# A mixture-of-experts stage with its gate steps ahead of its up steps, and constant multiplications where TensorE stands idle

## The chip, the cores and the metric

One core of one Trainium2 chip. The metric is the device time of one execution in microseconds (us), as the median of several. The engines are named as in the profile: PE is TensorE, PEld its weight loads, DVE is VectorE, ACT is ScalarE, POOL is GpSimd, SP is SyncE, which issues most of the DMAs.

## What is computed

Two layers of a hybrid decoder for 512 new prompt positions and 8 decode tokens (520 rows of width 1024), all in float32. Each layer adds attention and convolution, and then a mixture of experts:

```python
x += W_out [ DiffAttn(h) || ConformerConv(h) ],   h = RMSNorm(x)
x += HierMoE(RMSNorm(x))

# HierMoE: each row takes the best of 4 groups, and in it the best 2 of 4 experts
hg = x @ w_gate[e]            # 1024 -> 512
hu = x @ w_up[e]              # 1024 -> 512
y  = (silu(hg) * hu * gate_weight) @ w_down[e]   # 512 -> 1024
```

There are 16 experts. Each has three matrices of 2,048 KB, which are read from HBM once in each layer.

## The kernel before, in words

The kernel is written engine by engine: each engine has its own instruction stream, in which the order is written out by hand, and the streams meet at semaphores only. Both layers run through one loop (`l`).

**Tiles.** Rows are held in 5 tiles of up to 128 (the last has the 8 decode rows). Outputs of PE go to 8 banks of 128x512 float32 numbers. The expert stage works on 13 **units**. A unit is one expert with up to 128 rows, or, for units 2, 6 and 11, a pair of experts with up to 64 rows each, whose multiplications write the upper and the lower half of the same bank.

**Routing.** PE turns the last tile and multiplies it with the router's weights (L957). DVE picks groups and experts and signals `m_ok`. PE then makes cumulative counts (L976, L978), DVE makes one-hot rows from them, PE makes row lists from these (`early_list` L987 for the first two units, `unit_list` L996 for all of them), DVE turns the lists into row numbers (L1918), and POOL gathers the rows of units 0 and 1 (L1406). `gathered(u)` on PE waits for a gather and turns the rows (transposes, all recorded at L645, the helper `turn`); DVE multiplies them with the norm's weights into `probs` (L1456, the helper `tt`).

**A unit on PE.** `gate_up(u, ks)` (L1016) runs the steps `ks` out of 8: in each step one 128x512 multiplication for gate and one for up (twice as many, half as high, for a pair), all at L1027. At its first step it waits for `xt_ok` and for all gate and up loads of the unit. After its last step a 1x1 multiplication (L1032, the **fence**) signals `gu_ps`. ACT then computes Silu of the gate bank (L1335), DVE multiplies it by the up bank (`hidden`), PE turns the product (`turn_hidden`, four transposes), ACT copies it (L1339), and `down(u)` runs 4 steps of two multiplications (L1054) and a fence (L1060). ACT and DVE scale its two banks by the gate weight (L1347, L2012), and POOL adds the rows into `x_rows` in HBM (L1417), one addition after the other; a pair needs two.

The order on PE, after unit 0, is for each u: steps 0 to 3 of unit u+1, `turn_hidden(u)`, steps 4 to 7 of unit u+1, `gathered(u+2)`, `down(u)`. Unit 0's steps are interleaved with the row lists, and `gathered(1)` stands in their middle. DVE reaches `hidden(0)` only after it has made the row numbers of all units and the lists of rows that did not fit (`spill`, L2041).

**Weights.** SP issues the 48 loads of a layer in a fixed order (L520): gate and up of each expert of a unit, then its down matrices. There are 9 slots (`ring` 0 to 5, `w_last`, `x`, `feat`), and load n goes into slot n mod 9. A load is issued when `slot_used` tells that PE has done its last multiplication from the slot; SP waits for this in order, so a load whose slot isn't free holds back all behind it. Then come the next layer's projection weights.

**Layer's end.** PE reads the number of spilled rows (none here), and waits for `layer_go`, which POOL signals after the last row addition. SP then reloads `x`, and PE's next work is to turn small parameter rows and the normed tiles.

**Bank 5**, into which the change writes, is the up bank of units 1, 3, 5, 7, 9 and 11 and an output of earlier stages.

Of the kernel before, what the change touches and what calls it, by code (L numbers as in the profile page):

```python
# [31 lines left out]
KC = D // P  # L32
# [16 lines left out]
F = 512  # L49
# [9 lines left out]
UNITS = SINGLES + (EXPERTS - SINGLES) // 2  # L59
# [14 lines left out]
def places_of(u):  # L74

    q = u + sum(1 for pair in PAIRED if pair < u)
    return [q, q + 1] if u in PAIRED else [q]
# [20 lines left out]
def slot_of(q, j):  # L98

    return loads_in_order().index((q, j)) % SLOTS_MOE  # L100
# [96 lines left out]
def hybrid_step(nc, a, o, x_rows, xn_rows):  # L197
# [17 lines left out]
    with ExitStack() as ctx:  # L215
# [3 lines left out]
        def sem(name):  # L219
            return ctx.enter_context(nc.semaphore(name))  # L220
# [11 lines left out]
        const = sb("const", [P, const_width])  # L232
# [6 lines left out]
        ones = cs("ones")  # L239
# [24 lines left out]
        xe_t = probs_flat.rearrange("p (s c n) -> p s c n", s=2, n=P)  # L264
# [64 lines left out]
        bank = [pair_bank[i // 2][:, i % 2, :] for i in range(4)]  # L329
# [101 lines left out]
        xe_in = [sem("xe_in0"), sem("xe_in1")]  # L431
        xt_ps = sem("xt_ps")
        xt_ok = sem("xt_ok")
        gu_ps = sem("gu_ps")
        silu_ok = sem("silu_ok")
        hid_ok = sem("hid_ok")
# [34 lines left out]
        def halves_of(u):  # L471

            return [slice(0, HALF), slice(HALF, P)] if u in PAIRED else [slice(0, P)]
# [168 lines left out]
        def _(pe):  # L642
# [10 lines left out]
            with pe.Fori(0, DEPTH) as l:  # L653
# [8 lines left out]
                for t in range(TILES):  # L662
                    pe.wait_ge(xn_ok, l * TILES + (1, 2, 3, 5, 4)[t])
                    for g in range(2):
                        b = 4 + 2 * (t % 2) + g
# [250 lines left out]
                def project(t, ks):  # L916
                    if t == 0 and ks[0] == 0:
                        pe.wait_ge(slot_in[5], l * 16 * loads_of(5) + 16)
                        pe.wait_ge(ot_ok, l * SAMPLE + SAMPLE - 1)
                    if t == SAMPLE - 1 and ks[0] == 0:  # L920
                        pe.wait_ge(ot_ok, l * SAMPLE + SAMPLE)
                    if t == SAMPLE and ks[0] == 0:
                        pe.wait_ge(dec_f, l + 1)
                    if t >= 2 and ks[0] == 0:
                        pe.wait_ge(x2_ok, l * TILES + t - 1)
                    for k in ks:
                        w = ring[:, 5, :] if k < 4 else w_last
                        if t == 0 and k == 4:
                            pe.wait_ge(last_in, l * 16 + 16)
                            pe.wait_ge(cat_ok, l + 1)  # L930
                        for j in range(2):
                            mm = pe.matmul(bank[2 * (t % 2) + j][rows_at(t, j), :], feat[:, k, cols(t)],  # L932
                                           w[:, (k % 4) * D + j * AW:(k % 4) * D + (j + 1) * AW],
                                           start=(k == 0), stop=(k == KC - 1))
                            if t == TILES - 1 and k == 3 and j == 1:
                                mm.then_inc(slot_used[5], 1)
                    if ks[-1] == KC - 1:
                        mm.then_inc(wo_ps, 1)
# [15 lines left out]
                def route(t):  # L954
# [3 lines left out]
                                       w_route[:, k, :], start=(k == 0), stop=(k == KC - 1))  # L958
                    mm.then_inc(log_ps, 1)

                project(0, range(KC))
                sampled_turn()
                turn_o(SAMPLE - 1)
# [7 lines left out]
                route(TILES - 1)  # L971


                pe.wait_ge(m_ok, l + 1)
                width = TILES * EXPERTS
                pe.matmul(bank[7][:, 0:width + EXPERTS], cs("before"), chosen, start=True, stop=True)  # L976
# [6 lines left out]
                def early_list(u):  # L983

                    pe.wait_ge(hot_ok, l * LISTS + u + 1)
                    for t in range(TILES):
                        mm = pe.matmul(bank[1][:, u * PAY:(u + 1) * PAY], hot[:, u % 2, t, :], pay[:, t, :],  # L987
                                       start=(t == 0), stop=(t == TILES - 1))
                    mm.then_inc(idx_ps, 1)
# [21 lines left out]
                def landed(q, j):  # L1011

                    s = slot_of(q, j)
                    pe.wait_ge(slot_in[s], l * 16 * loads_of(s) + 16 * (load_of(q, j) + 1))

                def gate_up(u, ks):  # L1016
                    b = u % 2
                    if ks[0] == 0:
                        pe.wait_ge(xt_ok, l * 2 * UNITS + u * 2 + 2)
                        for q in places_of(u):  # L1020
                            for j in range(2):
                                landed(q, j)
                    for k in ks:
                        for j in range(2):
                            for q, rows in zip(places_of(u), halves_of(u)):
                                s = slot_of(q, j)
                                mm = pe.matmul(bank[2 + 2 * b + j][rows, :], xe_t[:, b, k, rows],  # L1027
                                               slots[s][:, k * F:(k + 1) * F], start=(k == 0), stop=(k == KC - 1))
                                if k == KC - 1:
                                    mm.then_inc(slot_used[s], 1)  # L1030
                    if ks[-1] == KC - 1:
                        pe.matmul(bank[7][0:1, 0:1], ones[:, 0:1], ones[:, 0:1], start=True, stop=True)\  # L1032
                            .then_inc(gu_ps, 1)

                def turn_hidden(u):
                    pe.wait_ge(hid_ok, l * UNITS + u + 1)
# [4 lines left out]
                def down(u, ks=range(FC)):  # L1041
# [17 lines left out]
                    if ks[-1] == FC - 1:  # L1059
                        pe.matmul(bank[2 + 2 * b][0:1, 0:1], ones[:, 0:1], ones[:, 0:1], start=True, stop=True)\  # L1060
                            .then_inc(dn_ps, 1)

                for u in range(FIXED):
                    early_list(u)
                gathered(0)
                for u in range(FIXED):
                    unit_list(u)
                for k in range(KC):
                    gate_up(0, range(k, k + 1))
                    unit_list(FIXED + k)  # L1070
                    if k == KC // 2 - 1:
                        gathered(1)
                for u in range(FIXED + KC, UNITS):
                    unit_list(u)
                for u in range(UNITS):
                    if u + 1 < UNITS:
                        gate_up(u + 1, range(4))
                    if u + 1 < UNITS:
                        turn_hidden(u)
                        gate_up(u + 1, range(4, KC))  # L1080
                    if u + 2 < UNITS:
                        gathered(u + 2)
                    if u == UNITS - 2:
                        down(u, range(FC - 1))
                        turn_hidden(u + 1)
                        down(u, range(FC - 1, FC))
                    else:
                        down(u)


                pe.wait_ge(spill_ok, l + 1)
                pe.sem_inc(pe_tick, 1)
                n_spill = pe.value_load(sp_i[0:1, 0:1], min_val=0, max_val=MAX_SPILL)
# [38 lines left out]
        def _(act):  # L1132
# [10 lines left out]
            with act.Fori(0, DEPTH) as l:  # L1143
# [187 lines left out]


                def silu(u):
                    act.wait_ge(gu_ps, l * UNITS + u + 1)
                    act.activation(hid[:, u % 2, :], bank[2 + 2 * (u % 2)][:, :], ACT.Silu).then_inc(silu_ok, 1)  # L1335

                def hidden_out(u):
# [116 lines left out]
        def _(v):  # L1454
            def tt(out, in0, in1, op):
                return v.tensor_tensor(out, in0, in1, op)  # L1456
# [24 lines left out]
            with v.Fori(0, DEPTH) as l:  # L1481
# [522 lines left out]
                def hidden(u):  # L2004
                    b = u % 2
                    v.wait_ge(silu_ok, l * UNITS + u + 1)
                    tt(hid[:, b, :], hid[:, b, :], bank[3 + 2 * b][:, :], ALU.mult).then_inc(hid_ok, 1)

                def y_half(u):
# [107 lines left out]
```

## Time and profile before

| | |
|---|---|
| median of 3 runs | 1511.77 us (1511.41 to 1515.68) |
| profiled execution | 1512.05 us, of which the trace spans 1510.0 |
| PE busy | 1304.7 us (86%), 4730 instructions |
| DVE busy | 631.5 us (42%) |
| ACT, POOL busy | 230.9 us, 152.3 us |
| mean granted clock of PE | 0.92 |
| mean DMA rate | 210 GB/s |

All sums of terms are made against the profiled execution, 1512.05 us. Layer 0 is 0 to 757 us, layer 1 the rest; the expert stage of layer 0 runs from 424 to 740 us, that of layer 1 from 1172 to 1480. The granted clock is 1.00 at 2.4 GHz and 0.50 at 1.2 GHz. PE's multiplications overlap, so the length of one record is longer than the time from one to the next; times of a stage are read from the chain or from the start of the first to the start of what follows. One float32 multiplication is shown as two MATMUL records.

### The profile page before, as it was taken

Reading aid. Unit: us, or ns where it says so; the run is one execution under the profiler, and the core shown is the slowest. Engines: PE = TensorE matmul, PEld = TensorE weight load, DVE = VectorE, ACT = ScalarE, POOL = GpSimd, SP = SyncE. Lnnn points to the kernel's source line nnn. Section 1 sums busy time; section 2 is a strip of 40 time slices with the busy share of each in tenths; the row PEclk is TensorE's granted clock in tenths of the full one; section 3 lists DMA queues with packets and bytes.
Section 4 is the critical chain, followed back from the end, with each engine's and each line's share of the span. In section 5 each row is a group of like instructions: output and inputs, shape, how many; then the busy total and the mean of one; then the engine's idle time right before and its main releaser. Section 6 shows DMA issues by size and latency. Waiting matters only on the chain.

```text
span 1510.0 us, 15202 instructions
## 1 busy us (share of the span) xinstructions
PE 1304.7 (86%) x4730; PEld 632.1 (42%) x4730; DVE 631.5 (42%) x1272; ACT 230.9 (15%) x740; POOL 152.3 (10%) x79
## 2 busy tenths in 40 slices
PE   5999975889679999999569999657994899999993
PEld 3544433445333443444245444344453444444441
DVE  4579986532461110111046799866325511111100
ACT  2011323321100000000110123232301000000000
POOL 0002240000010111110100022400000001101001
PEclk9999996799889999999869999868997899999997
DMA  9501333375274998998870022324833759999973
GB/s 303 201 1 55 94 91 111 92 263 217 100 276 175 342 387 325 386 386 327 278 248 0 1 77 86 101 88 126 303 145 122 291 190 366 385 324 384 391 263 92
DMA packets 102125, 316.81 MB, mean 210 GB/s; under 512 B 10552, under 2 KB 11122, under 8 KB 101980
## 3 DMA queue, kind: packets, MB, share of 16 engines
q1 hardware_dynamic: 88576, 276.91, 49.4%
q0 software_dynamic: 8000, 24.26, 6.9%
q10 hardware_dynamic: 5468, 14.64, 2.6%
q8 instruction: 42, 0.69, 0.2%
q14 instruction: 39, 0.32, 0.1%
HBM read 292.75 MB, written 31.74 MB: 215 GB/s over the span
## 4 chain that ended last, share of the span: by engine, by line
PE 55%; DVE 18%; DMA 12%; DVEq 7%; issue 4%; SPq 1%; ACT 0%; POOLq 0%; POOL 0%; ACTq 0%
PE pair L1027 11%; PE pair L1054 9%; PE bank L1027 9%; PE pair L686 8%; PE pair L932 8%; DMA w_last<-in_w_up 6%; DVE conv L1568 4%; PE bank L645 3%; DVEq L1570 3%; DVE probs L1456 2%; DMA x_rows<-qk_t,rows_g 2%; DVE sc_dec L1629 2%; DVE conv L1552 1%; DMA ring<-in_w_up 1%; PE pair L805 1%
## 5 line engine op out<-in xcount | busy, mean ns | idle before, releaser
L1027 PE MATMUL pair<-ring,probs 128*128 128x512 f32 (+1 forms) x384 | 169.3, 629 | 9.5 <-DMA w_last<-in_w_up 7.3
L1456 DVE TENSOR_TENSOR probs<-bank,vec_g 128x512 f32<-128x512 f32 x52 | 33.5, 685 | 314.2 <-PE bank L645 314.2
L1027 PE MATMUL bank<-ring,probs 128*128 128x512 f32 (+1 forms) x352 | 147.2, 613 | 1.7 <-DMA w_last<-in_w_up 1.2
L686 PE MATMUL pair<-feat,ring 128*128 128x512 f32 x256 | 141.9, 648 | 0.9 <-DVE feat L1456 0.9
L717 PE MATMUL pair<-ring,feat 128*128 128x512 f32 (+1 forms) x320 | 135.2, 595 | 1.6 <-ACT v_rows L1194 1.6
L1054 PE MATMUL pair<-ring,v_rows 128*128 128x512 f32 (+1 forms) x320 | 126.9, 594 | 1.9 <-DVE qk_t L2012 1.9
L1390 POOL TENSOR_TENSOR w_last<-x 128x2048 f32<-128x2048 f32 x16 | 73.7, 4624 | 381.9 <-ACT x L1229 275.4
L1568 DVE SCALAR_TENSOR_TENSOR conv<-u_t,conv_w,conv 128x512 f32<-128x512 f32 x120 | 105.4, 919 | 5.2 <-issue 0.9
L1417 POOL DMA_INDIRECT x_rows<-qk_t,rows_g x32 | 49.6, 1550 | 520.6 <-DVE qk_t L2012 470.0
L1552 DVE SCALAR_TENSOR_TENSOR conv<-u_t,conv_w,conv 128x512 f32<-128x512 f32 x120 | 90.2, 751 | 17.2 <-issue 13.2
L1027 PEld LDWEIGHTS pair<-ring,probs 128*128 128x128 f32 (+1 forms) x384 | 61.7, 180 | 79.1 <-issue 71.3
L1027 PEld LDWEIGHTS bank<-ring,probs 128*128 128x128 f32 (+1 forms) x352 | 58.2, 182 | 75.8 <-issue 74.1
L2012 DVE TENSOR_SCALAR qk_t<-pair,gate 128x512 f32<-128x512 f32 x26 | 19.5, 751 | 166.8 <-PE pair L1060 90.9
L717 PEld LDWEIGHTS pair<-ring,feat 128*128 128x128 f32 (+1 forms) x320 | 50.4, 170 | 71.7 <-issue 71.6
L717 PE MATMUL bank<-ring,feat 128*128 128x512 f32 (+1 forms) x160 | 79.4, 592 | 0.0
L1054 PEld LDWEIGHTS pair<-ring,v_rows 128*128 128x128 f32 (+1 forms) x320 | 52.0, 180 | 63.9 <-issue 61.6
L687 PEld LDWEIGHTS bank<-feat,ring 128*128 128x128 f32 x256 | 49.5, 193 | 63.0 <-issue 63.0
L1406 POOL DMA_INDIRECT qk_t<-xn_rows,rows_g x26 | 28.1, 1080 | 439.1 <-DVE rows_g L1918 370.2
L932 PE MATMUL pair<-w_last,feat 128*128 128x512 f32 (+1 forms) x160 | 64.8, 592 | 0.0
L932 PE MATMUL pair<-ring,feat 128*128 128x512 f32 (+1 forms) x160 | 64.2, 597 | 0.0
L1054 PE MATMUL pair<-feat,v_rows 128*128 128x512 f32 (+1 forms) x128 | 56.9, 595 | 0.0
L645 PE MATMUL bank<-const,probs 128*128 128x128 f32 x144 | 27.2, 311 | 31.7 <-DVE probs L1703 31.7
(270 smaller groups left out, 1604.2 us busy)
## 6 DMA issues: line engine op xcount, KB each, us to landing
ring<-in_w_gate SPq DMA_DIRECT2D x24, 2048.0 KB, 21.1
ring<-in_w_up SPq DMA_DIRECT2D x22, 2048.0 KB, 21.6
ring<-in_w_down SPq DMA_DIRECT2D x20, 2048.0 KB, 12.9
ring<-in_w_in SPq DMA_DIRECT2D x10, 2048.0 KB, 14.5
x<-in_cache_k SPq DMA_DIRECT2D x64, 256.0 KB, 3.0
x<-in_cache_v SPq DMA_DIRECT2D x64, 256.0 KB, 2.9
feat<-in_w_down SPq DMA_DIRECT2D x8, 2048.0 KB, 21.1
w_last<-in_w_gate SPq DMA_DIRECT2D x6, 2048.0 KB, 15.9
```

Of the source, the lines that this page charges most:

```text
L645: return pe.transpose(dst, src, ident[0:rows, 0:rows])
L686: pe.matmul(main[:, :], w, feat[:, k, 0:SEQ], start=(k == 0), stop=(k == KC - 1))
L687: mm = pe.matmul(smp, w, feat[:, k, SEQ:TOK], start=(k == 0), stop=(k == KC - 1))
L717: mm = pe.matmul(dst[j][rows_at(t, j), :], feat[:, k, cols(t)], ring[:, j, k * AW:(k + 1) * AW], start=(k == 0), stop=(k == KC - 1))
L932: mm = pe.matmul(bank[2 * (t % 2) + j][rows_at(t, j), :], feat[:, k, cols(t)], w[:, (k % 4) * D + j * AW:(k % 4) * D + (j + 1) * AW], star ...
L1027: mm = pe.matmul(bank[2 + 2 * b + j][rows, :], xe_t[:, b, k, rows], slots[s][:, k * F:(k + 1) * F], start=(k == 0), stop=(k == KC - 1))
L1054: mm = pe.matmul(bank[j][rows, :], hid_t[:, b, k, rows], slots[s][:, k * D + j * F:k * D + (j + 1) * F], start=(k == 0), stop=(k == FC - 1))
L1390: pool.tensor_tensor(qk_prod[:, half, :, :], pages[:, half * 4:half * 4 + 4, :], q_rep[:, half:half + 1, :].to_broadcast([P, PAGES, AW]), ...
L1417: pool.indirect_dma_start(out=x_rows[:, :], out_offset=bass.IndirectOffsetOnAxis(ap=rows_g[0:n, at:at + 1], axis=0), in_=ye[0:n, b, :], in ...
L1456: return v.tensor_tensor(out, in0, in1, op)
L1552: v.scalar_tensor_tensor(acc, u_t[:, c, bass.ds(w, SEQ)], conv_w[:, c, bass.ds(w, 1)], acc, ALU.mult, ALU.add)
L1568: v.scalar_tensor_tensor(conv[:, k, 0:SEQ], u_t[:, k, bass.ds(w, SEQ)], conv_w[:, k, bass.ds(w, 1)], conv[:, k, 0:SEQ], ALU.mult, ALU.add)
```

## The change

`gate_up` becomes `gate_or_up`: a unit's 8 gate steps run first, then its 8 up steps. Only the gate part waits for the gate loads, only the up part for the up loads. Each part ends with a fence; the gate's signals a new semaphore, `gate_ps`, for which Silu now waits, and DVE's product waits for `gu_ps` as well. In the unit loop `turn_hidden(u)` stands between the gate and the up part of unit u+1. In unit 0 the two-multiplication steps between row lists become gate, gate for the first four and up, up for the last four.

Besides, PE gets `keep_warm(b, count)`: multiplications of the constant ones with 512 columns of constants into bank 5, whose result nothing reads: 8 ahead of the wait for `m_ok`, 1 ahead of the first list, 5 ahead of `gathered(0)`, and 14 after the last down stage.

```diff
+                def keep_warm(b, count):
+                    for _ in range(count):
+                        pe.matmul(bank[b][:, :], ones, const[:, 0:512], start=True, stop=True)
...
                 route(TILES - 1)
+                keep_warm(5, 8)
                 pe.wait_ge(m_ok, l + 1)
...
-                def gate_up(u, ks):
+                def gate_or_up(u, j, ks=range(KC)):
                     b = u % 2
                     if ks[0] == 0:
-                        pe.wait_ge(xt_ok, l * 2 * UNITS + u * 2 + 2)
+                        if j == 0:
+                            pe.wait_ge(xt_ok, l * 2 * UNITS + u * 2 + 2)
                         for q in places_of(u):
-                            for j in range(2):
-                                landed(q, j)
+                            landed(q, j)
                     for k in ks:
-                        for j in range(2):
-                            for q, rows in zip(places_of(u), halves_of(u)):
...
+                        for q, rows in zip(places_of(u), halves_of(u)):
...
                     if ks[-1] == KC - 1:
                         pe.matmul(bank[7][0:1, 0:1], ones[:, 0:1], ones[:, 0:1], start=True, stop=True)\
-                            .then_inc(gu_ps, 1)
+                            .then_inc(gu_ps if j else gate_ps, 1)
...
+                keep_warm(5, 1)
                 for u in range(FIXED):
                     early_list(u)
+                keep_warm(5, 5)
                 gathered(0)
                 for u in range(FIXED):
                     unit_list(u)
                 for k in range(KC):
-                    gate_up(0, range(k, k + 1))
+                    gate_or_up(0, k // 4, range(2 * k % KC, 2 * k % KC + 2))
                     unit_list(FIXED + k)
...
                     if u + 1 < UNITS:
-                        gate_up(u + 1, range(4))
+                        gate_or_up(u + 1, 0)
                     if u + 1 < UNITS:
                         turn_hidden(u)
-                        gate_up(u + 1, range(4, KC))
+                        gate_or_up(u + 1, 1)
...
+                keep_warm(5, 14)
                 pe.wait_ge(spill_ok, l + 1)
...
                 def silu(u):
-                    act.wait_ge(gu_ps, l * UNITS + u + 1)
+                    act.wait_ge(gate_ps, l * UNITS + u + 1)
...
                 def hidden(u):
                     v.wait_ge(silu_ok, l * UNITS + u + 1)
+                    v.wait_ge(gu_ps, l * UNITS + u + 1)
```

## Rows read from the trace of the kernel before

**Rows 1.** The page's part 2: the span in 40 slices, tenths busy

```profile
PE   5999975889679999999569999657994899999993
PEclk9999996799889999999869999868997899999997
```

**Rows 2.** Waits of PE, layers 0 and 1: us in total, times, longest

```profile
PE pair L1027 <- DMA w_last<-in_w_up: 3.9, 1, 3.9
PE bank L645 <- DVE v_rows L1456: 3.8, 1, 3.8
...
PE bank L1027 <- DMA w_last<-in_w_up: 0.6, 1, 0.6
...
PE pair L1027 <- DMA w_last<-in_w_up: 3.3, 1, 3.3
...
PE bank L1027 <- DMA ring<-in_w_up: 0.5, 1, 0.5
```

**Rows 3.** The chain that ended last: start us, us, what

```profile
569.49 9.46 PE pair L1027 x32
578.95 0.59 PE bank L645 x4
579.54 7.02 PE pair L1027 x32
586.55 0.12 PE bank L1032 x2
...
587.84 6.87 PE pair L1054 x16
594.71 0.12 PE bank L1060 x2
...
1317.77 8.78 PE pair L1027 x32
```

**Rows 4.** Windows: length, busy us of each engine, PEclk, DMA share, GB/s

```profile
400.00:401.00 1.00, 0.00 (x0) 0.00 (x0) 0.89 (x4) 0.17 (x1) 0.00 (x0) 0.62 0.00 0
427.00:428.00 1.00, 1.00 (x12) 0.34 (x11) 0.00 (x0) 0.00 (x0) 0.00 (x0) 0.73 1.08 434
567.00:568.00 1.00, 0.00 (x0) 0.00 (x0) 0.04 (x1) 0.00 (x0) 0.70 (x1) 0.74 1.03 410
540.00:560.00 20.00, 20.00 (x59) 9.34 (x58) 2.63 (x4) 1.88 (x3) 2.63 (x2) 1.00 1.03 390
1178.00:1179.00 1.00, 1.00 (x3) 0.37 (x2) 0.00 (x0) 0.00 (x0) 0.00 (x0) 0.76 0.99 406
460.00:480.00 20.00, 20.00 (x67) 8.40 (x67) 2.63 (x4) 1.28 (x2) 2.66 (x2) 0.96 0.21 72
```

**Rows 5.** Timeline of PE: start us, us, line, shape, count, idle before and its end

```profile
407.91 0.74 PE L976 MATMUL bank<-conv,const 128*128 128x96 f32 x2 [9.98 <-DVEq L1887]
408.44 2.21 PE L978 MATMUL bank<-conv,const 128*128 128x80 f32 x10
412.33 0.29 PE L987 MATMUL pair<-conv 128*128 128x10 bf16 x5 [1.68 <-DVE conv L1456]
...
419.88 1.98 PE L645 MATMUL bank<-const,qk_t 128*128 128x128 f32 x8 [6.52 <-DMA qk_t<-xn_rows,rows_g]
...
424.00 3.71 PE L1027 MATMUL pair<-ring,probs 128*128 128x512 f32 x4 [1.08 <-DVE probs L1456]
...
1172.40 3.75 PE L1027 MATMUL pair<-ring,probs 128*128 128x512 f32 x4 [1.08 <-DVE probs L1456]
```

**Rows 6.** Timeline of DVE ahead of the first gate step

```profile
421.01 1.56 DVE L1456 TENSOR_TENSOR conv<-const,conv 128x640 bf16<-128x640 f32 x2 [0.15 <-issue]
422.49 1.28 DVE L1456 TENSOR_TENSOR probs<-bank,vec_g 128x512 f32<-128x512 f32 x2
```

**Rows 7.** Timeline of all engines at the layer change

```profile
749.74 1.55 POOL L1417 DMA_INDIRECT x_rows<-qk_t,rows_g  x1 [6.03 <-DMA x_rows<-qk_t,rows_g]
761.72 0.28 PE L645 MATMUL pair<-const,probs 29*128 29x29 f32 x1 [22.09 <-issue]
```

More of the change, by code:

```diff
@@ L433, in hybrid_step @@
         xt_ok = sem("xt_ok")
+        gate_ps = sem("gate_ps")
         gu_ps = sem("gu_ps")
@@ L1014, in landed @@
                     pe.wait_ge(slot_in[s], l * 16 * loads_of(s) + 16 * (load_of(q, j) + 1))
-                def gate_up(u, ks):
+                def gate_or_up(u, j, ks=range(KC)):
                     b = u % 2
                     if ks[0] == 0:
-                        pe.wait_ge(xt_ok, l * 2 * UNITS + u * 2 + 2)
+                        if j == 0:
+                            pe.wait_ge(xt_ok, l * 2 * UNITS + u * 2 + 2)
                         for q in places_of(u):
-                            for j in range(2):
-                                landed(q, j)
+                            landed(q, j)
                     for k in ks:
-                        for j in range(2):
-                            for q, rows in zip(places_of(u), halves_of(u)):
[L1026 to L1030, printed above, removed]
+                        for q, rows in zip(places_of(u), halves_of(u)):
+                            s = slot_of(q, j)
+                            mm = pe.matmul(bank[2 + 2 * b + j][rows, :], xe_t[:, b, k, rows],
+                                           slots[s][:, k * F:(k + 1) * F], start=(k == 0), stop=(k == KC - 1))
+                            if k == KC - 1:
+                                mm.then_inc(slot_used[s], 1)
                     if ks[-1] == KC - 1:
                         pe.matmul(bank[7][0:1, 0:1], ones[:, 0:1], ones[:, 0:1], start=True, stop=True)\
-                            .then_inc(gu_ps, 1)
+                            .then_inc(gu_ps if j else gate_ps, 1)
                 def turn_hidden(u):
```

## The prediction

> **What bounds the kernel now.** I read the page's slices first [rows 1]: TensorE (PE) is busy in nearly every slice, except where routing runs (around 410 and 1160 us) and at the layer change (740 to 780 us). Its granted clock is below full around the same places, and once more inside each expert stretch. So time can be won in two ways: fewer waits of PE, and fewer microseconds at 1.2 GHz.
>
> Next the waits of PE in the two expert stretches [rows 2]. A wait on a DMA of up weights costs 3.9 us in layer 0 and 3.3 us in layer 1; there are small ones of 0.6 us in each layer and one of 0.5 us in layer 1. The chain [rows 3] shows what a long one is: PE starts the first gate/up step of unit 6 (a pair of experts, four loads) at 569.49, after 3.9 us of waiting (so from 565.6), when the fourth load, the second expert's up, is there. The wait costs twice, since the half stage behind it takes 9.46 us where the next, equal one takes 7.02; in layer 1 it is 8.78 against 7.02 [rows 3]. The granted clock fell to half just before those steps [rows 4]. The DMA engines are full there, at 390 GB/s [rows 4]: a load of 2,048 KB (2.10 MB) takes 5.4 us, and if loads land in the order of issue, as one queue suggests, each lands about 5.4 us behind the one before.
>
> Last the PE's own order in the routing stretch and at the layer change [rows 5, 7], and what VectorE (DVE) does meanwhile [rows 6].
>
> **The gate/up split: what it removes.** A step of two multiplications prints four records [rows 5], so a multiplication is two records, and a half stage of 16 records is 8 of them in 6.87 us (the down stage at 587.84 is such a one, [rows 3]): 0.86 us each at 2.4 GHz. Before, the first step of a unit waits for all its gate and up loads. After, it waits for the gates, and 8 multiplications, the fence and the four transposes lie ahead of the first up step: 7.0 + 0.1 + 0.6 = 7.7 us.
> At unit 6 the third load (the second gate) lands near 569.4 - 5.4 = 564.0, ahead of 565.6; gates start at once. The ups are asked for at 573.3, and the last landed by 569.5. So the wait of 3.9 goes, and with it the slow clock behind it, 9.46 - 7.02 = 2.4. Layer 1: 3.3 and 8.78 - 7.02 = 1.8. The small waits, all on up loads and under 7.7 us, go as well: 0.6; 0.6 and 0.5. Layer 0: 3.9 + 2.4 + 0.6 = 6.9; layer 1: 3.3 + 1.8 + 0.6 + 0.5 = 6.2; together 13.1 us off. All of it is on the path, since PE is what the chain follows there.
> What is late next: unit 7's gate. From 565.6 with no wait, PE needs 7.02 + 0.12 + 0.59 + 7.02 + 0.12 + 1.17 + 6.87 + 0.12 = 23.0 us and asks for it at 588.6. Three loads follow the up of 569.4, so it lands at 569.4 + 16.2 = 585.6 at the earliest. At the latest it lands at 589.4: the kernel before starts unit 7 at 594.83, 0.12 us behind the fence at 594.71, so without a wait [rows 3], and the up that it also needed is one load behind the gate. Between no wait and 0.8; I take none. Unit 7's ups are then asked for at 596.3, after 594.83. The gate's slot is free some 7.7 us earlier, but SyncE issues loads strictly in order and the next one mostly waits for a down slot, so I give that nothing.
>
> **What it adds.** One more 1x1 fence per unit: 13 units in 2 layers, 26 in all, 0.12 us each as the one at 586.55 [rows 3], on PE's path: 3.1 us back. Number and length of the real multiplications and weight loads stay. ScalarE runs Silu during the up steps, and DVE's product waits for up as well, as it did: the hidden rows are asked for a down stage and a half stage later, and nobody waits for them. The exception is unit 0, where PE waits 3.8 us for DVE [rows 2]; DVE gets to it only behind its row lists and spill lists, not behind Silu, so it stays. No DMA is added or moved in its queue. Balance: 13.1 - 3.1 = 10.0 us off.
>
> **The constant multiplications.** Each is a real 128x512 one of 0.86 us at 2.4 GHz, and 1.86 at 1.2 GHz (3.71 for two, [rows 5]). What they stand in front of, and the cover:
> 8 behind the router, 6.9 us in an idle time of 9.98 [rows 5]. The cumulative counts wait on DVE, which is untouched; cover left 3.1 us.
> 1 ahead of the first list: 0.9 in 1.68 of idle. 5 ahead of the first gather's transposes: 4.3 in 6.52; cover left 2.2.
> 14 at the layer's end: 12.0 in 22.09 [rows 7]. They end near 751.6, and PE is next needed at 761.72, when the third row addition (issued at 749.74) and the reload are through. Behind the router the clock fell some 2.3 us into an idle time (400.24 in [rows 4], idle from 397.93); with 10 us of idle left here it falls as well, so I give these nothing, and at the kernel's end nobody waits for PE. Cost of all 28 per layer: nothing, while PE has its full clock in them.
> What they can give: the counts, 407.91 to 410.65, run at half clock (2.7 us) and would take 1.4. The transposes of the first gather gain nothing, since DVE's first product of features starts at 422.49, straight behind DVE's own work of 421.01 to 422.57 [rows 6]. The first gate steps run at half clock from 424.00 to 427.5 in layer 0 and from 1172.40 to 1178.5 in layer 1 [rows 4, 5]: 1.8 and 3.0 us. Upper end: 2 x 1.4 + 1.8 + 3.0 = 7.6 us. Lower end: nothing, or a loss of 1 us per layer where the five run at half clock (8.6 to 9.3 us in 6.52, of which DVE hides some 1.5). Against those 2.3 us of idle ahead of the fall, 3.1 and 2.2 us of idle with only small work between are at the edge. I take 3.0, nearer to the lower end.
> The Trainium skill, "TensorE: Matmul & The Clock Gate", Part 4, says that transposes do not count as work for the clock. By that rule the stretch from the last of the five to the first gate step would count as idle, the steps would start at half clock all the same, and the sum would keep of the 3.0 only what the counts give. The rows here cannot decide it: the transposes at 419.88 ran in a clock that was low before them.
>
> **Sum:** 1512.05 - 10.0 - 3.0 = 1499.05 us against the profiled execution; the median of the runs is 0.3 below that one, so 1498.8, say 1499.
>
> **Rivals.**
> A. The filler does not carry the clock to the gate steps. For it: 4 to 5 us between the fifth filler and the first gate step hold only transposes and small lists. It leaves the split's 10.0 and about 1 us of counts, less up to 1: 1501 to 1503. The Trainium skill's rule on transposes, above, would make it so. Chance 0.2.
> B. The waits only move: DMA is full at unit 6 [rows 4], so unit 7's gate or a later load comes late by what was won. For it: 390 GB/s at that point; against it: from 460 to 480 us the DMA engines are 21% busy [rows 4], so over a layer they have time to spare, and the bound worked out for unit 7. Of 13.1 us then some 4 are left, less 3.1 of fences and with 3 from routing: 1508. Chance 0.13.
> C. Slower: the fillers overrun. They are in PE's in-order queue; at 1.86 us each the eight take 14.9 in 9.98 (4.9 late), the one and the five another 2, the fourteen 26.0 in 22.09 (3.9 late, layer 0 only): 2 x 6.9 + 3.9 = 17.7 late, less the split's 10.0: 1520. It decides once a filler costs more than some 1.65 us, where the late parts reach 10. Against it: the clock is full when the eight and the fourteen start [rows 1, 4], and a multiplication's two records already follow each other into one bank at 0.43 us. Chance 0.06.
> D. More than forecast: the fillers hold the clock all through routing (7.6) and the wait at unit 0 no longer drops it: 1492 to 1495. Chance 0.1.
> My forecast, 1496 to 1501: 0.51.
>
> **Numbers.** Point 1499. Range 1493 to 1508: it leaves out C and the edges of B and D. A measurement can tell about 0.3% (4.5 us) from no change: faster takes the forecast, A, D and a little of B: 0.83; within it most of B: 0.11; slower 0.06.
>
> **What the profile after would show.** Step by step: no wait on an up load in either layer, the half stages of unit 6 at 7.0 us both, and no fall of the clock ahead of them; if a wait on a gate load of unit 7 stands there instead, B. Extra fences of 0.12 us, 26 of them. Eight fillers ending 3 us ahead of the counts; the counts in 1.4 us, not 2.7; the first step of unit 0 in 1.8 us, not 3.7 (if 3.7, A). PE idle for 10 us at the layer change and the clock low there. The step most open is the clock between 405 and 424 us. I would be wrong if loads landed later than before, or if the hidden rows became late.

## The result, and the profile after

The changed kernel takes 1501.72 us (median of 5 runs, 1496.11 to 1503.67) against 1511.77 in the same comparison (1509.77 to 1515.68): a ratio of 0.9922, 95% interval 0.9895 to 0.9948, so 8 to 16 us faster. The profiled execution took 1502.65 us with a span of 1500.6, against 1512.05 and 1510.0; PE's mean granted clock is 0.935, after 0.92. The forecast was 1499. Executions more than 1.5% above the fastest of their kernel (three in the comparisons below, at clocks of 0.43 to 0.72) are left out of every ratio and interval.

The longer waits of PE in the expert stretches of layer 0 and, behind "...", of layer 1 (us in total, times, longest):

```profile
PE bank L646 <- DVE v_rows L1465: 2.2, 1, 2.2
PE bank L646 <- DMA qk_t<-xn_rows,rows_g: 2.1, 1, 2.1
PE pair L1033 <- DVE probs L1465: 1.0, 1, 1.0
...
PE bank L646 <- DVE v_rows L1465: 2.1, 1, 2.1
```

No wait on a load of up weights is left in either layer (3.9, 3.3 and the small ones in [rows 2]), and no other wait on a load has come in their place. The chain at unit 6 shows the same from the other side (start us, us, what):

```profile
563.85 0.12 PE pair L1066 x2
563.97 7.02 PE pair L1033 x32
570.99 0.12 PE bank L1038 x2
571.11 0.59 PE bank L646 x4
571.69 7.02 PE pair L1033 x32
...
579.99 6.87 PE pair L1060 x16
586.86 0.12 PE bank L1066 x2
586.98 7.06 PE bank L1033 x16
```

Gate part and up part take 7.02 us both, where the first half stage took 9.46 [rows 3]: no wait, no slow clock behind it. Unit 7 starts at 586.98, 0.12 us behind the start of the fence, so its gate had landed: by the trace at 586.17, only 0.8 us before. Unit 6 is a pair: from its gate part's start to its up part's start it is 7.02 + 0.12 + 0.59 = 7.72 us.

The routing stretch on PE:

```profile
397.84 0.65 PE L958 MATMUL bank<-w_route,feat 128*8 128x20 f32 x16 [0.28 <-DVE feat L1465]
398.42 8.62 PE L965 MATMUL bank<-const 128*128 128x512 f32 x16
408.43 0.46 PE L983 MATMUL bank<-conv,const 128*128 128x96 f32 x2 [1.40 <-DVEq L1896]
408.73 1.21 PE L985 MATMUL bank<-conv,const 128*128 128x80 f32 x10
...
412.49 4.54 PE L965 MATMUL bank<-const 128*128 128x512 f32 x10
419.17 1.23 PE L646 MATMUL bank<-const,qk_t 128*128 128x128 f32 x8 [2.14 <-DMA qk_t<-xn_rows,rows_g]
...
423.19 3.78 PE L1033 MATMUL pair<-ring,probs 128*128 128x512 f32 x4 [0.97 <-DVE probs L1465]
```

The counts take 1.5 us from their first start to their end, after 2.7 [rows 5]; none of the fillers makes its successor late; and the first gate step still takes 3.78 us, as slow as the 3.71 before. Its clock (length, busy us of each engine, PEclk, DMA share):

```profile
398.00:399.00 1.00, 1.00 (x17) 0.85 (x14) 0.15 (x1) 0.06 (x1) 0.00 (x0) 0.51 0.74 258
...
401.00:402.00 1.00, 1.00 (x3) 0.53 (x2) 0.77 (x5) 0.65 (x1) 0.00 (x0) 0.78 0.21 29
...
417.00:418.00 1.00, 0.03 (x1) 0.00 (x0) 1.00 (x1) 0.00 (x0) 0.32 (x1) 1.00 0.30 103
...
421.00:422.00 1.00, 0.36 (x8) 0.28 (x9) 1.00 (x3) 0.00 (x0) 0.00 (x0) 0.96 1.06 410
422.00:423.00 1.00, 0.21 (x5) 0.13 (x5) 1.00 (x3) 0.00 (x0) 0.00 (x0) 0.50 0.94 381
```

The clock was full from 401.4 to 421.9, and fell 1.3 us ahead of the step that it was kept for.

To compare executions I cut each trace at the first record of the same piece of work. Worked from the timelines, in us (the last column is the whole span; "units 0, 1" runs from the first gate step to the first down step, "units 1 to 12" from there to the end of the last down stage):

```
                     counts        units 0, 1      units 1 to 12    attention   span
                    L0    L1       L0     L1       L0      L1      L0     L1
before             4.42  4.42    43.39  43.40    272.11  271.42  293.5  290.6  1510.0
changed            3.19  3.19    41.75  43.34    267.52  267.52  293.9  294.1  1500.6
split alone        4.42  4.42    41.12  43.56    267.52  267.52  292.9  295.5  1502.9
fill alone         3.19  3.19    41.33  40.38    272.92  270.69  295.0  296.0  1510.5
fill alone, again  3.19  3.19    41.31  41.14    270.19  272.00  293.7  295.6  1506.6
no gate fence      3.19  4.43    43.47  43.39    265.15  265.16  294.0  293.7  1498.6
two gate fences    3.19  3.19    43.71  40.76    268.07  268.07  294.1  293.6  1500.7
no fences          3.19  3.20    42.67  42.34    263.28  263.47  293.7  294.2  1493.0
bridge             3.19  3.19    41.88  41.74    267.52  267.52  294.2  295.7  1500.3
product first      3.19  3.19    39.45  39.25    267.52  267.52  295.0  294.4  1495.2
both of these      3.19  4.43    35.22  36.91    267.52  267.52  294.7  295.2  1490.5
all three          3.19  3.19    34.18  34.17    263.57  263.65  290.4  294.3  1473.5
```

"counts" is from the first count to the first list; "attention" is from the layer's first projection to the output projection, which no kernel here touches. Of the 9.4 us between the two profiled executions, 8.5 are in units 1 to 12 (4.6 and 3.9), 2.5 in the counts, 1.7 in units 0 and 1; attention gave back 3.9, 3.5 of them in layer 1, and the stretches left out of the table make up the rest (0.6). The 3.9 us of attention are not the change's: that column moves by 5.6 us over all these kernels with the same instructions in it. The 1.7 us of units 0 and 1 are not clearly the fillers' either, as layer 0 of the split alone has 41.12 without any.

### The profile page after: what moved, and what is told of

Same layout as the page of the kernel before. It is cut to its first block, busy times and chain, and to the rows that moved or that the text cites. A ratio compares the mean times of both kernels' runs of the same rounds, so it can differ in the third digit from the quotient of the medians.

```text
span 1500.6 us, 15538 instructions
## 1 busy us (share of the span) xinstructions
PE 1367.5 (91%) x4894; PEld 655.1 (44%) x4894; DVE 631.8 (42%) x1272; ACT 228.4 (15%) x740; POOL 152.5 (10%) x79
## 4 chain that ended last, share of the span: by engine, by line
PE 65%; DVE 19%; DVEq 7%; issue 4%; DMA 3%; SPq 1%; ACT 0%; POOLq 0%; ACTq 0%
PE pair L1033 13%; PE pair L1060 12%; PE bank L1033 10%; PE pair L687 9%; PE pair L933 8%; PE bank L646 4%; DVE conv L1577 4%; DVEq L1579 3%; DVE probs L1465 2%; DVE sc_dec L1638 2%; DVE conv L1561 2%; PE pair L806 1%; DMA x_rows<-qk_t,rows_g 1%; DVE u_t L1465 1%; PE pair L809 1%
## 5 line engine op out<-in xcount | busy, mean ns | idle before, releaser
L1033 PE MATMUL pair<-ring,probs 128*128 128x512 f32 (+1 forms) x384 | 163.6, 612 | 2.0 <-DVE probs L1465 2.0
L1356 ACT ACTIVATE qk_t<-pair,gate 128x512 f32<-128x512 f32 x26 | 17.9, 687 | 331.3 <-PE pair L1066 186.6
```

## The experiments

**Split alone and fill alone.** The changed kernel without its 56 fillers:

```diff
-                keep_warm(5, 8)
...
-                keep_warm(5, 1)
...
-                keep_warm(5, 5)
...
-                keep_warm(5, 14)
```

> The changed kernel without any of its constant multiplications: gate steps first, nothing else. Theory (fences cost more than their own record, 0.27 us instead of 0.12, and the fillers give only the warm counts, 1.3 us a layer, as the first gate step starts 1.3 us earlier behind the counts): about 2.7 us slower than the changed kernel, so 7 us faster than before; the counts run at half clock (2.7 us), the expert stage behind the first down stage takes 259 us as in the changed kernel. Rival (the fillers carry more than that, by the clock in the steps of units 0 and 1): 5 us or more slower than the changed kernel. Rival (the fillers give nothing): equal to it.

Measured: 1506.84 us, ratio to before 0.9958 (0.9944 to 0.9973), 5 us slower than the changed kernel by the medians. Units 1 to 12 take 267.52 us in both layers (not 259), to the last digit the changed kernel's: the split alone makes that. The counts are back at 4.42. The traces explain 2.5 us of the 5, all of it in the counts, as the theory says; units 0 and 1 together are no longer than in the changed kernel (84.7 and 85.1 us), so the place that the rival named shows nothing. The timed 5 us are the rival's size, but the intervals of the two ratios overlap and don't separate the two.

The kernel before with the fillers, twice:

```diff
+                keep_warm(5, 8)
                 pe.wait_ge(m_ok, l + 1)
...
+                keep_warm(5, 1)
                 for u in range(FIXED):
                     early_list(u)
+                keep_warm(5, 5)
...
+                keep_warm(5, 14)
                 pe.wait_ge(spill_ok, l + 1)
```

> The kernel before with the constant multiplications alone. Theory: 2 to 3 us faster than before, all of it in the cumulative counts (1.5 us instead of 2.7, in each layer); the waits on up loads at unit 6 stay at 3 to 4 us. Rival (fillers overrun or disturb): equal or slower. Rival (fillers shift the stream so that the up waits shrink too): 5 us or more faster.

> The kernel before with the fillers alone, once more, since the first comparison gave 5 to 12 us with one profile at its slow end. Theory (the fillers are worth the counts, 2.5 us, and the rest of that was the clock in other stages, which differs from execution to execution): the ratio lies between 0.996 and 0.999. Rival (they are worth 5 us or more in the timed runs): 0.994 to 0.996 again.

Measured: 0.9943 (0.9921 to 0.9966) the first time, with runs from 1496 to 1513 us, and 0.9988 (0.9976 to 1.0001) the second, 1506 to 1514 us. The two intervals do not meet, so the timed worth of the fillers is only bounded: between nothing and 12 us. The first has the size of the rival's 5 us or more, and the second is in the theory's range. What both traces show is the same 1.23 us per layer in the counts, and 2.1 to 3.0 us less in units 0 and 1, which the theory didn't expect. The long wait on the up load at unit 6 stays in both. The first trace has, in layers 0 and 1:

```profile
PE pair L1033 <- DMA w_last<-in_w_up: 3.8, 1, 3.8
...
PE pair L1033 <- DMA w_last<-in_w_up: 3.4, 1, 3.4
```

and the second 3.4 us in either layer. So the fillers do nothing for the waits on loads, and the rival by which the up waits would shrink falls. The rest of their timed worth is not explained; the clock of stages that differs from execution to execution is one place where it can sit. The 2.1 us in units 0 and 1 need not be theirs: layer 0 of the split alone, without fillers, has 41.12 us too.

These two traces also show that the slow clock behind a wait is not certain. In layer 0 of the second one PE waits 3.4 us at unit 6 and the clock stays full (length, busy us, PEclk, DMA share):

```profile
560.00:580.00 20.00, 16.61 (x74) 5.86 (x74) 1.35 (x2) 1.28 (x2) 2.62 (x2) 1.00 1.03 387
```

From the start of one down stage to the next it is 26.35 us there and 29.27 in the kernel before. Layer 1 of the first one is alike. So of six such waits of 3.3 to 3.9 us (two in each of three traces without the split), four were followed by a slow clock.

**The price of a fence.** Silu waits for the signal that the last gate multiplication gives to its slot anyway:

```diff
+        def last_used(eng, l, u, j):
+
+            q = places_of(u)[-1]
+            s = slot_of(q, j)
+            eng.wait_ge(slot_used[s], l * loads_of(s) + load_of(q, j) + 1 + (1 if s < SLOTS else 0))
...
-                    if ks[-1] == KC - 1:
+                    if ks[-1] == KC - 1 and j == 1:
                         pe.matmul(bank[7][0:1, 0:1], ones[:, 0:1], ones[:, 0:1], start=True, stop=True)\
-                            .then_inc(gu_ps if j else gate_ps, 1)
+                            .then_inc(gu_ps, 1)
...
-                    act.wait_ge(gate_ps, l * UNITS + u + 1)
+                    last_used(act, l, u, 0)
```

> The changed kernel without the 26 new fences: Silu waits for the gate slot's own signal of its last multiplication. Theory (a fence ahead of the hidden transposes costs 0.27 us, by the unit period of 22.91 us against 22.64 before): 26 x 0.27 = 7 us faster than the changed kernel, unit period back at 22.64. Rival (the fence costs its 0.12 us only, and the longer period is of the eight steps into one bank): 3 us faster, period 22.79.

Measured: 1496.43 us, ratio 0.9884 (0.9858 to 0.9911), 5.3 us below the changed kernel. Units 1 to 12 take 265.15 us: 2.37 less for the 11 gate fences in them, 0.215 each. All 26 are then worth 5.6 us, if those of units 0 and 1 cost as much. The theory's figures return for units of one expert: 22.91 us from one down stage to the next in the changed kernel, 22.64 here and before.

> The changed kernel with a second 1x1 multiplication ahead of each gate fence. Theory (the first fence costs 0.12 for itself and 0.15 by making the transposes behind it start as after a pause): the second adds only its own 0.12, 3 us slower in all. Rival (each one costs 0.27): 7 us slower.

A second fence ahead of the first: 1501.76 us, 0.9917 (0.9893 to 0.9941), equal to the changed kernel; 268.07 us, so 0.05 for each second fence. The 3 us of the theory couldn't be told from nothing in the timed runs; the trace shows that neither it nor the rival was right. Side by side, without a gate fence:

```profile
497.34 7.13 PE L1038 MATMUL bank<-ring,probs 128*128 128x512 f32 x16
504.31 0.60 PE L651 MATMUL bank<-const,v_rows 128*128 128x128 f32 x4
504.75 7.03 PE L1038 MATMUL bank<-ring,probs 128*128 128x512 f32 x16
```

and with two:

```profile
497.79 7.13 PE L1033 MATMUL bank<-ring,probs 128*128 128x512 f32 x16
504.85 0.19 PE L1039 MATMUL bank<-const 128*1 128x1 f32 x2
504.90 0.19 PE L1040 MATMUL bank<-const 128*1 128x1 f32 x2
505.02 0.66 PE L646 MATMUL bank<-const,v_rows 128*128 128x128 f32 x4
505.51 7.03 PE L1033 MATMUL bank<-ring,probs 128*128 128x512 f32 x16
```

This is a unit of one expert. From the start of one part to the start of the next it is 7.41 us without and 7.72 with two (7.67 with one, in the changed kernel). The first fence starts 7.06 us behind the part's start where the transposes start after 6.97, and the transposes behind it hold PE for 0.49 us, not 0.44. So it costs before itself, for itself and behind itself, 0.26 us in all; a second one adds 0.05, less than the 0.12 of the theory and the 0.27 of the rival. For a pair of experts it is different. The chain of the last kernel of this section, which has no fence there, at unit 11, the last pair:

```profile
664.40 7.02 PE bank L1037 x32
671.42 0.59 PE bank L650 x4
672.00 7.02 PE bank L1037 x32
```

7.60 us here and 7.72 in the changed kernel, at unit 11 as at unit 6 above: 0.12. The transposes cost a pair 0.59 us with or without it. Eight units of one expert at 0.26 and three pairs at 0.12 are 2.4 us, what was measured. From down stage to down stage it is 0.27 in seven of the eight and 0.14 at unit 7: without the fences PE comes to that unit just before its gate load has landed, at 588.38 us in layer 0, and starts it with that landing:

```profile
588.42 7.13 PE bank L1038 x16
```

Without the up fences as well (VectorE's product waits for the up slot's signal):

> The changed kernel without gate and up fences: Silu and the product wait for the slots' own signals. Theory (a fence ahead of transposes costs 0.215 us, as the gate's does in the last comparison, 2.37 us over 11 units): the stretch from the first down stage to the last one's end takes 265.15 - 2.4 = 262.8 us, and the kernel is 10 to 11 us faster than the changed one. Rival (it costs 0.12 or less behind the up steps, where the gather's transposes follow): 263.9.

Measured: 1495.71 us, 0.9879 (0.9855 to 0.9902); units 1 to 12 in 263.28 and 263.47 us, 4.2 and 4.1 below the changed kernel, between theory (262.8) and rival (263.9). The timed gain over it, 6 us, falls short of the 10 that I expected; the traces differ by 7.6. The stretch hides what an up fence costs, since a wait on a gate load, at unit 7, has come in its place, 1.0 us in layer 0 and 1.2 in layer 1:

```profile
PE bank L1037 <- DMA ring<-in_w_gate: 1.0, 1, 1.0
...
PE bank L1037 <- DMA ring<-in_w_gate: 1.2, 1, 1.2
```

In the units without such a wait the up fence costs more than the gate's: from down stage to down stage a unit of one expert takes 22.31 us after 22.64, 0.33 less, and a pair 0.12 less.

**The gap ahead of the first gate step.** Two more fillers per layer, one behind the transposes of the first gather and one behind two lists:

```diff
                 gathered(0)
+                keep_warm(5, 1)
                 for u in range(FIXED):
                     unit_list(u)
+                keep_warm(5, 1)
```

> The changed kernel with two more constant multiplications per layer in the gap ahead of the first gate step: one behind the first gather's transposes, one behind the first two unit lists. Theory (the clock falls there because transposes and small lists alone do not hold it): the clock stays full into the first gate step, which takes 1.9 us for two multiplications instead of 3.8, and 1.5 to 2.5 us per layer are won up to the last list; but unit 0's hidden rows wait for DVE, which follows the last list, so this is kept; 3 to 5 us faster than the changed kernel. Rival (the fall is not from that gap): first step still 3.8 us, time equal.

Measured: 1502.4 us, 0.9924 (0.9907 to 0.9942): no gain. But the clock did as the theory said:

```profile
423.98 1.98 PE L1033 MATMUL pair<-ring,probs 128*128 128x512 f32 x4
...
443.38 7.13 PE L1033 MATMUL bank<-ring,probs 128*128 128x512 f32 x16
450.44 0.19 PE L1038 MATMUL bank<-const 128*1 128x1 f32 x2
454.49 1.11 PE L646 MATMUL bank<-const,v_rows 128*128 128x128 f32 x4 [3.86 <-DVE v_rows L1467]
455.39 9.35 PE L1033 MATMUL bank<-ring,probs 128*128 128x512 f32 x16
```

The first step takes 1.98 us. Then PE waits 3.86 us for VectorE's product, the clock falls in that wait, and the up part of unit 1 takes 9.35 us. Units 0 and 1 together: 41.88 us after 41.75. What the first step won was given back 30 us later. Layer 1 is alike: a first step of 1.98 us, and 41.74 us for the two units.

**Transposes as filler.** The first eight fillers replaced by 47 transposes of a constant:

```diff
-                keep_warm(5, 8)
+                for _ in range(47):
+                    turn(bank[5][:, 0:P], ident, P)
```

> The changed kernel with its first eight constant multiplications replaced by 47 transposes of 128x128 constants, of the same length (0.146 us each at full clock, 6.9 us). Theory (transposes do not hold the clock): it falls within them and is at half when the counts start, which take 2.7 us instead of 1.5; the transposes then last up to 12 us and make the counts late by 1 to 3 us per layer. Rival (transposes hold it like multiplications): counts in 1.5 us, time equal to the changed kernel.

Measured: 1505.0 us, 0.9941 (0.9921 to 0.9962). The transposes run from 398.02 to 405.04, with nothing else on PE. Their clock:

```profile
399.00:400.00 1.00, 1.00 (x6) 1.00 (x5) 0.00 (x0) 0.00 (x0) 0.00 (x0) 0.50 0.00 0
400.00:401.00 1.00, 1.00 (x7) 1.00 (x6) 0.93 (x3) 0.00 (x0) 0.00 (x0) 0.50 0.08 16
401.00:402.00 1.00, 1.00 (x8) 1.00 (x7) 0.70 (x5) 0.77 (x1) 0.00 (x0) 0.66 0.15 25
402.00:403.00 1.00, 1.00 (x11) 1.00 (x10) 0.72 (x4) 0.73 (x2) 0.00 (x0) 1.00 0.05 8
```

It rose from half to full while transposes were all that ran. The split alone, with nothing in this place, is the comparison: there the clock fell at 397.6 us and stayed at half until 428.4. So the theory fell: float32 transposes count as work. They took 7.0 us with 3.4 of them at half clock, so they were shorter than I had planned them, and the counts were not late. Yet the clock fell again at 408.5, 0.2 us into the counts, which took 4.28 us to the first list. In layer 1, where the transposes ran at full clock, it fell too, ahead of the counts, and they took 4.43. Ahead of the counts PE was idle for 3.27 and 4.6 us. The idle time, not their kind, is the likely cause, though not the shown one: with the eight multiplications and 2.9 to 3.2 us of idle time the clock fell in two layers and stayed in three.

**The fourteen at the layer's end.**

```diff
-                keep_warm(5, 14)
```

> The changed kernel without the fourteen constant multiplications at the layer's end. Theory: nothing, within 1 us; the stretch from the last down stage's end to the next layer's first projection stays at 38 to 40 us, and the clock is at half there in either case. Rival (they warm the next layer's start): 2 us or more slower.

Measured: 1502.9 us, 0.9925 (0.9904 to 0.9946), equal to the changed kernel. From the end of the last down stage to the next layer's first projection it is 39.5 us without them and 39.3 with them. They are worth nothing, and cost nothing. The low clock there began at 749.6 us instead of 736.9, but still held when the projection began.

**The wait at unit 0.** VectorE's first product ahead of its 8 us of spill lists instead of behind them:

```diff
+                hidden(0)
+
                 S = MAX_SPILL
...
-                    if u < UNITS - 1:
+                    if 0 < u < UNITS - 1:
                         hidden(u)
```

> The changed kernel with VectorE's first product (unit 0's hidden rows) put ahead of its spill lists instead of behind them. Theory (the wait of 2 to 4 us at unit 0 is VectorE's 8 us of spill lists, and the clock falls in it): PE no longer waits at unit 0, the stretch from the first gate step to the first down stage falls from 42 to 37 or 38 us in each layer, and the kernel is 7 to 9 us faster than the changed one. Rival (VectorE's work returns as a wait elsewhere, as the spill lists then stand ahead of the features of unit 2): 3 us or less.

Measured: 1496.44 us, 0.99 (0.9883 to 0.9916), 5.3 us below the changed kernel by the medians, less than the 7 to 9 expected and more than the rival's 3. The wait is gone, and no other has come for it; units 0 and 1 take 39.45 and 39.25 us, 6.4 less in all, but not the 37 or 38 expected, since their first steps and the first part of unit 1 still meet a slow clock, as this one, behind the small lists:

```profile
446.92 8.82 PE L1033 MATMUL bank<-ring,probs 128*128 128x512 f32 x16
455.67 0.19 PE L1038 MATMUL bank<-const 128*1 128x1 f32 x2
455.79 0.66 PE L646 MATMUL bank<-const,v_rows 128*128 128x128 f32 x4
```

> Both: the product ahead of the spill lists and the two bridging multiplications. Theory (the bridge's gain, 1.8 us a layer in unit 0's steps, was lost only in the wait for VectorE): the same stretch takes 35 to 36 us, 2 us a layer less than with the product first alone; 11 to 13 us faster than the changed kernel. Rival (the bridge is worth nothing in itself): equal to the product first alone.

With the two bridging fillers besides: 1488.05 us, 0.9847 (0.9828 to 0.9866). Units 0 and 1 take 35.22 and 36.91 us, 4.2 and 2.3 less than with the product first alone. The theory's 2 us fit layer 1; in layer 0 the slow clock behind the small lists (447.4 to 450.8 us) is missing as well, about which the edit does nothing, so that part may be chance. The same two fillers that were worth nothing in the changed kernel are worth 8.4 us here by the medians, 6.6 of them in this stretch.

> The two of them without the gate and up fences. Theory: the terms add, 4.1 us less per layer from the first down stage on and some more in units 0 and 1: 20 us faster than the changed kernel, about 1481 to 1483 us. Rival (with PE faster, the DMA becomes the bound and waits on loads return): 1486 or more, with waits on gate loads at units 7 or 11 in the trace.

With the fences gone too: 1477.7 us (1475.36 to 1482.08), ratio 0.9789 (0.9769 to 0.9809), 33 us faster than the kernel before and 24 faster than the changed one, more than the 20 expected. Its attention is 5.2 us shorter than the last kernel's, both layers together, which is not the edit's doing. Units 1 to 12 take 263.6 us, and the wait on unit 7's gate load stands in each layer, as without the fences alone:

```profile
PE bank L1037 <- DMA ring<-in_w_gate: 1.2, 1, 1.2
```

It is a gate load, as the rival said, but 1.2 us of it, and not the 1486 us or more: at this unit PE has come up with the loads.

## Why the prediction was right or wrong

**The split: right, to a tenth against this trace.** I took 6.9 us off layer 0 and 6.2 off layer 1 ahead of the fences. The kernel without gate fences shows the split by itself: 272.11 - 265.15 = 6.96 and 271.42 - 265.16 = 6.26 us. The wait went, the slow clock behind it went, the small waits went, and unit 7's gate was there in time. The landings bear the working out: in the kernel before, the second gate of unit 6 landed at 564.32 (I had 564.0) and the gate of unit 7 at 588.41, inside my 585.6 to 589.4 and 0.2 us ahead of the 588.6 at which I had PE ask for it. So rival B was nearer than its chance of 0.13 suggests; it begins once the fences are gone (1.0 to 1.2 us). The slot's earlier release brought nothing: unit 7's gate load is issued 1.2 us behind PE's arrival at unit 6 in both kernels. That the sum holds to a tenth has some luck in it. 4.2 of the 13.1 us are the slow clock behind the two waits, and in two of six such waits it did not come. Against the two traces of the fillers alone the same split is worth 5.0 to 7.8 us a layer.

**The fences: the term that was mis-sized.** I priced 26 at 0.12 us, the piece of the chain that a fence has, 3.1 us together. They cost 0.215 each on average, 5.6 us. The row that I took it from, the fence at 586.55, belongs to a pair and stands behind an up part; for a pair the price is right, and 20 of the 26 units are of one expert, where the fence also lengthens what is around it. I gave this term no upper bound at all. The 2.5 us look like the 2.7 between 1499 and 1501.7, but that is no account of them. In the profiled executions 9.4 us were won, not 13.0: 2.0 less than forecast in units 1 to 12, which are the fences; 1.7 more than forecast in the counts and units 0 and 1, with the few fences there; and 3.9 lost in attention, which the change doesn't touch, less 0.6 in the rest.

**The fillers as cost: right.** All four groups ended ahead of what they stood in front of; the overrun of rival C did not come. The eight took 8.62 us instead of 6.9, since the clock fell at 398.0, 0.4 us before they began, during the small multiplications of the router; the cover of 3.1 us paid for it, of which 1.4 were left.

**The fillers as gain: the forecast's step was wrong here, rival A right.** The counts gave 1.23 us per layer of the 1.4 that I had as the most, 2.5 together. The first gate steps gave nothing: 3.78 us. I had taken 3.0 for both out of 7.6, so the sum was near, but by other parts than a mixture of the two. Rival A (chance 0.2, 1501 to 1503) named the place and holds the measured 1501.7. That its number fits is luck: it allowed about 1 us for the counts, which gave 2.5, and the fences and attention made up for it. The reason beside it, the Trainium skill's statement in "TensorE: Matmul & The Clock Gate", Part 4, that transposes are no work for the clock, does not hold here, as the 47 transposes show (0.50 to 1.00 at 401.7 us). There was just little work in the gap: from 417.0 to 423.2 PE worked for 1.2 us on transposes and 0.6 on lists. Two more fillers closed it, in all six layers that have them (first steps of 1.98 us). The yardstick that I held against the gaps, 2.3 us of idle time ahead of the fall behind the router, was no yardstick: in the split alone, with the same work there, the clock fell 0.6 us before the router's multiplications ended in layer 0 and 2.3 us behind them in layer 1.

**"So it stays" for the wait at unit 0: right, and dearer than I saw.** I left its 3.8 us alone (2.2 are left in the changed kernel, since the gate part ahead of it ran into a slow clock instead, 8.82 us after 7.10); it is also what makes a gain ahead of it worthless, as the bridge showed. I had put the case of a kept clock (D) at 1492 to 1495 with that wait no longer slowing the clock. The bridge kept the clock through the first steps and won nothing; 1488 was reached only when the wait itself was taken away.

**The end of the layer: right.** Nothing, as forecast.

What stays open: the timed worth of the fillers alone, since the two comparisons of the same kernel disagree, and why split and fill together are 5 us faster than the split alone by the medians, where the traces account for 2.5. Open is also where in a stretch the clock falls: the same instructions met it at different times from execution to execution.

## What to carry to other kernels

Splitting a step that waits for two loads into two that wait for one each pays the wait, and the slow clock behind it where there is one, if the first half is longer than the gap between the landings; here 6.96 us for 6.9 worked out. Then look which load is the next to be late, and by how little it isn't: here 0.8 us. Signal from an instruction that is there anyway: a tiny multiplication whose only use is to signal cost 0.26 to 0.33 us in a stream of full multiplications, more than twice its own piece of the chain. And before filling an idle stretch to hold the clock, look for the next wait behind it: two fillers were worth nothing ahead of a wait of 3.9 us, and 8 us by the medians once VectorE's order was changed.

## What the runs showed of the hardware that was not expected

- A 1x1 multiplication ahead of transposes costs 0.26 us in a stream of full multiplications where its piece of the chain says 0.12, and 0.12 in a stream of half-height pairs; a second one beside it costs 0.05. The fences behind the up parts cost 0.33 and 0.12.
- The clock can fall while PE is at work: at 398.0 us PE was in the router's multiplications of 20 columns, behind an idle time of 0.28 us, and the window from 398 to 399 us is 1.00 busy at a clock of 0.51. In the split alone it fell at the same place, 0.6 us before they ended; in the kernel before, 2.3 us behind their end. It rose again at 401.4.
- Float32 transposes alone raised the granted clock from 0.50 to 1.00.
- A wait of 3.4 us left the clock full in two layers, and four others of 3.3 to 3.9 us were followed by a clock of 0.50.
- Attention, the same instructions in every kernel here, took from 290.4 to 296.0 us. The clock was low for 48 and 51 us in the two shortest and for 75 and 71 in the two longest. A gain of 2 to 3 us in another stage is read from that stage's rows, not from one span.
